# Two vector instructions of the mixing step moved behind the next remainder, in a Trainium2 transformer block

## The reference

```python
hn = rms_norm(h, norm_mlp_g[l])
u = jnp.square(jax.nn.relu(hn @ w_mlp_in[l]))   # 2048 -> 8192
h = h + u @ w_mlp_out[l]                         # 8192 -> 2048
```

## Time and profile before

| | us |
|---|---|
| median of three runs | 2722.47 |
| lowest, highest | 2721.12, 2723.18 |
| the profiled execution | 2723.25 |
| its span in the trace | 2721.5 |
| PE busy | 2560.5 (94%) |
| DVE busy | 1713.7 (63%) |
| POOL busy | 1023.0 (38%) |
| ACT busy | 976.9 (36%) |

### The profile page before, as it was taken

The page is one execution under the profiler, slowest core; times in us unless marked ns, Lnnn a source line. Parts: engine busy times, 40 slices in busy tenths (PEclk is TensorE's granted clock), DMA queues, the critical chain, the costliest instruction groups (busy, mean ns, idle before and its releaser), DMA issues.

```text
span 2721.5 us, 34691 instructions
## 1 busy us (share of the span) xinstructions
PE 2560.5 (94%) x14354; PEld 2219.9 (82%) x14354; DVE 1713.7 (63%) x1894; ACT 976.9 (36%) x1246; POOL 1023.0 (38%) x560
## 2 busy tenths in 40 slices
PE   9999999999999999997999999999789888989886
PEld 8898888888888888887999999999777666767665
DVE  5565555455333334345666665666798999899888
ACT  4445443344222223123433333333343334333434
POOL 0000000000000000017777777777756577565743
PEclk9999999999999999998999999999899999999988
DMA  7222222222323334222443334333523332322221
GB/s 246 84 88 80 92 80 88 89 82 85 101 92 100 92 100 155 94 84 70 127 129 124 125 120 137 119 124 123 224 78 140 117 131 78 139 93 113 104 85 70
DMA packets 158064, 299.49 MB, mean 110 GB/s; under 512 B 8512, under 2 KB 113104, under 8 KB 149088
## 3 DMA queue, kind: packets, MB, share of 16 engines
q1 hardware_dynamic: 157776, 297.44, 32.5%
q10 hardware_dynamic: 144, 0.02, 0.0%
HBM read 276.41 MB, written 21.01 MB: 109 GB/s over the span
## 4 chain that ended last, share of the span: by engine, by line
PE 60%; DVE 22%; issue 7%; POOL 5%; ACT 3%; DMA 1%; SPq 0%; DVEq 0%; ACTq 0%; POOLq 0%
PE bank L1473 20%; PE bank L1475 19%; PE bank L1474 19%; DVE ring L1282 8%; DVE up_lo L1214 4%; POOL down_raw L1376 4%; DVE stream L1307 2%; ACT up_hi L782 2%; DVE down_forms L1273 2%; DVE hidden_out L1237 1%; PE bank L1579 1%; ACT ring L834 1%; PE bank L1562 1%; POOL up_raw L1376 1%; DMA up_raw<-in_up_units 1%
## 5 line engine op out<-in xcount | busy, mean ns | idle before, releaser
L1376 POOL TENSOR_TENSOR up_raw<-up_raw 128x256 f32<-128x256 f32 (+1 forms) x384 | 515.1, 1345 | 194.6 <-DMA up_raw<-in_up_units 173.9
L901 DVE TENSOR_TENSOR w_lo<-landing,w_hi 128x1024 fp32r<-128x1024 f32 x200 | 248.8, 1244 | 467.4 <-ACT w_hi L593 467.2
L1376 POOL TENSOR_TENSOR down_raw<-down_raw 128x1024 f32<-128x1024 f32 x128 | 385.7, 3031 | 265.6 <-DVE ring L1282 265.6
L1282 DVE TENSOR_TENSOR ring<-down_raw,ring 128x1024 fp32r<-128x1024 f32 x224 | 439.0, 1974 | 67.3 <-ACT ring L834 66.1
L1214 DVE TENSOR_TENSOR up_lo<-up_raw,up_hi 128x1792 fp32r<-128x1792 f32 x128 | 301.3, 2354 | 244.2 <-ACT up_hi L782 244.2
L1379 POOL TENSOR_TENSOR form_raw_a<-form_raw_a 128x1024 f32<-128x1024 f32 x3 | 8.1, 2730 | 1184.9 <-DVE form_raw_a L1185 1184.9
L593 ACT ACTIVATE w_hi<-landing 128x1024 fp32r<-128x1024 f32 x200 | 212.0, 1060 | 667.5 <-PE bank L1475 663.5
L834 ACT ACTIVATE ring<-down_raw 128x1024 fp32r<-128x1024 f32 x224 | 234.0, 1058 | 464.6 <-PE bank L1475 247.6
L782 ACT ACTIVATE up_hi<-up_raw 128x1792 fp32r<-128x1792 f32 x128 | 218.0, 1703 | 437.9 <-PE bank L1475 401.7
L1473 PE MATMUL bank<-xn_hi,w_hi 128*128 128x512 f32 x928 | 367.1, 396 | 2.8 <-DVE w_lo L901 2.2
L1475 PE MATMUL bank<-xn_hi,w_lo 128*128 128x512 f32 x928 | 361.8, 390 | 0.0
(11 more groups left out here) (167 smaller groups left out, 5257.9 us busy)
## 6 DMA issues: line engine op xcount, KB each, us to landing
up_raw<-in_up_units SPq DMA_DIRECT2D x128, 512.0 KB, 3.6
down_raw<-in_down_blocks SPq DMA_DIRECT2D x64, 1024.0 KB, 6.8
landing<-in_w_in SPq DMA_DIRECT2D x72, 512.0 KB, 3.6
landing<-in_w_gate SPq DMA_DIRECT2D x64, 512.0 KB, 3.7
landing<-in_w_out SPq DMA_DIRECT2D x32, 512.0 KB, 3.6
hidden_rows<-hidden_out SPq DMA_DIRECT2D x32, 512.0 KB, 5.3
raw_forms<-hidden_rows SPq DMA_DIRECT2D x17, 512.0 KB, 10.2
landing<-in_w_branch_a SPq DMA_DIRECT2D x16, 512.0 KB, 3.4
```

The source lines that it names most:

```text
L901: nc.vector.tensor_tensor(w_lo[:, s, :], landing[:, u % LAND, :], w_hi[:, s, :].bitcast(F32), ALU.subtract).then_inc(unit_lo, 1)
L1282: nc.vector.tensor_tensor(part[:, 1, :], raw, part[:, 0, :].bitcast(F32), ALU.subtract)\
L1376: return nc.gpsimd.tensor_tensor(out, a, b, ALU.add)
```

## The change

The mixing is cut in two. `mixed_products` holds its waits and the first four instructions. `hidden` keeps the last two: the fifth subtraction (L1233 before) and the squared ReLU (L1237 before). `mixed_products` stays where the whole was, behind the remainder of unit u+2. `hidden` is issued one step of the loop later, behind the remainder of unit u+3. For the last group, in the down stage, both stand together as before. No instruction is added or taken away.

```diff
-            def hidden(s):
+            def mixed_products(s):
                 done = 5 * s
                 dve.wait_ge(up_used, up_place(s, 3) + 1)
...
                 dve.wait_ge(mixed, done + 3)
                 nc.vector.tensor_tensor(mix[:, 1:3, :], up_products(s, 2, 7, 4), mix[:, 5:7, :], ALU.add)\
                     .then_inc(mixed, 1)
-                nc.vector.tensor_tensor(mix[:, 3:4, :], fifth, mix[:, 6:7, :], ALU.subtract).then_inc(mixed, 1)
-                dve.wait_ge(mixed, done + 5)
+
+            def hidden(s):
+
+                nc.vector.tensor_tensor(mix[:, 3:4, :], up_products(s, 3, 4), mix[:, 6:7, :], ALU.subtract)\
+                    .then_inc(mixed, 1)
+                dve.wait_ge(mixed, 5 * s + 5)
                 if s:
                     dve.wait_ge(hidden_stored, 16 * s)
                 nc.vector.scalar_tensor_tensor(out=hidden_out[:], in0=mix[:, 0:4, :], scalar=0.0, in1=mix[:, 0:4, :],
...
                 if UP_ORDER[n - 2][1] == 3:
-                    hidden(UP_ORDER[n - 2][0])
+                    mixed_products(UP_ORDER[n - 2][0])
+                if n > 2 and UP_ORDER[n - 3][1] == 3:
+                    hidden(UP_ORDER[n - 3][0])
...
                     if p == 2:
+                        mixed_products(SUBS - 1)
                         hidden(SUBS - 1)
```

## The result

| | before | after |
|---|---|---|
| median of three runs, us | 2722.47 | 2698.19 |
| lowest, highest | 2721.12, 2723.18 | 2696.33, 2700.52 |
| span of the profiled execution | 2721.5 | 2698.7 |

The ratio is 0.9912, with a 95% interval of 0.989 to 0.9935: 24.3 us less.

The account below looks back on a forecast made before the run. PE was taken to bound the up stage, stalling on late DVE remainders: 18.4 us of waits, 24.9 with added cost, less 1.5, plus 1.0, gave 24.4 us off 2723.25, 2698.9 profiled; 2698 us on the median's scale, range 2694 to 2702.

Parts of the forecast that it names:

- The remainder of u+3 starts on ACT's high parts, 0.86 us earlier: Up stage, DVE: with two instructions gone ahead of it, this remainder waits for ACT, starting at 1605.93 instead of 1606.79.
- It takes 2.02 us, since POOL's sum now comes second: Remainder of u+3 starts before POOL's sum of u+5, ends at 1607.95; PE wants it at 1608.97, so the stall goes.
- Rival 1: POOL's sum of u+5 still starts first, remainder takes 3.1 us: 5 us back, 2703 us; chance 0.12.
- The moved instructions are covered: DVE behind the remainder of u+3: 0.41 + 1.40 us fit before u+4's remainder can start at 1610.95; cost 0.
- POOL's sums of u+5 end near 1603.9: POOL's three sums, each held by a DVE instruction, end near 1613.7 in the prediction's frame; ACT wants them at 1614.26.
- SP's store is the same: SP's queue: the store starts when the ReLU ends, 1609.8 to 1610.5, against 1610.22 before; its longer wait holds nobody.
- The sum, 24.4 us: Up stage total: 18.4 us of PE waits plus 25 x 0.26, less 1.5, plus 1.0 from the stretch before.
- POOL's late sums: PE's longest wait, 1.2 us, was put down to these and expected to stay: 1.2 + 0.26 us off the gain.
- a ceiling: Whole excess of both up-stage stretches, 27.0 us, which no version of this change can pass in this stage.
- the slower rival: POOL's queue past its margin in every group: 47 us lost against 24 won, 2745 us; chance 0.03.
- the priced row: ACT's wait for a late set of POOL sums, 5.01 us instead of 3.33: 1.68 us as the price of one.
- the 0.5 us of one set of sums: Margin left for POOL's sums of u+5 before ACT wants them; it was 4 us with the stall.

Follow-up runs that it names:

- run 5: Kernel before, mixing where it was, with POOL's sums of u+5 made to wait until the remainder of u+3 is done: 2700.89 us (0.9914).
- run 8: Changed kernel with POOL's first sum of u+5 made three times, 2 x 1.3 us more of POOL per group: 2751.82 us (1.0098).
- run 6: Changed kernel, POOL's first sum of u+4 made twice: 2708.72 us; second kernel also leaves out one block's sum in three units per group: 2698.84 us.

## Why the prediction was right

It forecast 2698 us, and the changed kernel came to 2698.19 and, a second time, 2697.49. Step by step:

- *The remainder of u+3 starts on ACT's high parts, 0.86 us earlier:* right, with 0.90 us of idle DVE ahead of it. The run with the ReLU alone moved shows that this is all the change needs.
- *It takes 2.02 us, since POOL's sum now comes second:* right, and decisive. The old order with POOL held gives nearly the whole gain; the old amount of mixing in one place, one unit later, gives nothing. The stall of 1.01 us was 0.86 us late plus 1.09 held, less the 1.02 in hand, and 0.1 us between the first two matmuls behind it. Taking either away ends it: the hold in run 5, the lateness in run 8, where a remainder on time was held for 1.05 us and cost 0.13. That is why 0.86 us of earlier start is worth a whole stall. (By the starts in the earlier trace rows the remainder was 0.78 us late and POOL's sum 0.21 us ahead of it; the prediction's 0.86 and 0.29 count from the end of the squared ReLU, 0.08 us later. Nothing hangs on it.)
- *Rival 1* (the remainder of u+3 still held) did not come about: it took 2.02 or 2.03 us in all 28 groups of the first profile.
- *The moved instructions are covered:* right. They ended at 1600.37, where I had 1600.7 in this frame. The margin was thin: one more squared ReLU there cost 15.2 us in the stretch.
- *POOL's sums of u+5 end near 1603.9* (in this frame): too late by 2.1 us, they ended at 1601.79. The third sum came ahead of the remainder of u+4, and not behind it. The mistake was harmless: the remainder paid 0.5 us of its margin.
- *SP's store is the same:* right for its issue. Its landing I left out: the median went from 5.3 to 2.9 us, and the load of u+6 is now issued some 2 us ahead of it and not right beside it. The other runs fit that: 5.3 us with POOL held, where load and store are issued together, 2.9 with all six moved, where they aren't.
- *The sum, 24.4 us:* its size was off. The stage gave 27.0 us in the first pair and 27.2 in the second. The term is "25 waits with 0.26 us each, less one of POOL's". It left out what the list of waits doesn't hold of the stretch's excess: PE was late at u+3 in 27 of the 28 groups, where the list has 25 waits in all. And it kept 1.5 us for POOL's late sums that were not POOL's. The longest wait, 1.2 us, is that of unit 118, whose remainder begins at 1881.55, is held to 3.11 us and is a u+3 like the others; the unit behind POOL's late sums cost only 0.4 us. All of it went. The excess of 27.0 us, which I had taken for a ceiling, was the value. The first pair's medians show 24.3 us; the second time, against the kernel before as timed beside it, they show 26.6.
- That 24.3 us was measured where 24.4 had been worked out was therefore partly luck: the sum was 2.6 us short of what the stage gives. In the first pair of profiles 4.2 us of the stage's 27.0 don't reach the span, 2.9 of them at the start of the up stage, at a granted clock of 0.82 instead of 0.87. The forecast lies between the first pair's 22.8 us of span and the second's 27.5.

Of the slower rival, the priced row (1.68 us for a late set of sums) was of the right order: two extra sums cost 1.88 us per group and lose to the kernel before. But its margin was measured by the wrong thing. From the 0.5 us of one set of sums that I worked out, or the 2.7 us that the first profile shows (they end at 1601.79, and ACT takes them at 1604.46), one can't tell where losses begin; the runs put that at about 0.9 us of added POOL work per group, and the point where the whole gain is lost between 1.3 and 2.6 us.

## What to carry to other kernels

When a stall is the sum of two delays less a margin, taking out either delay is worth the whole stall, as long as the other is not much longer than the margin (1.05 us held against 1.0 in hand cost 0.13). So work out the margin first, and put the work that can wait (here a squared ReLU, wanted only by a store) behind the instruction that PE wants next, but no more of it in one place than the gap there holds. Here the excess of a stretch over its back-to-back time was a better forecast (27.0 us, measured 27.0 and 27.2) than the sum of the waits in the list (24.4).

## What the runs showed of the hardware

- An engine's waits are not its room. POOL waited 2.8 us per group for its loads, and 1.3 us more work already made it the bound, with waits down to 0.2 us in the whole stretch. A POOL sum that comes second to a DVE instruction with both inputs in SBUF is stretched (2.44 us beside the remainder, 1.29 alone): POOL's busy time went from 467.5 to 555.6 us for 28 sums that take 1.3 us alone, 36 us.
- In the rows of this case, the instruction that starts first runs on, and the other takes nearly as much longer as the first still needs. For the remainder of 2.02 us, the time still needed and the time added were 1.23 and 1.09 us in the kernel before, 0.63 and 0.49 in the changed kernel, 0.34 and 0.20 in the second kernel of run 6. The squared ReLU, 1.3 to 1.4 us without such a start, took 1.86 with 0.78 us still to go. The rule cited in the prediction (the Trainium skill, "SBUF — State Buffer", section "SBUF: two separate sides") agrees. The five mixing instructions, which read one input from PSUM, took the same 0.41 to 0.69 us with a POOL sum beside them and without.
- Who comes first at the port is decided within a tenth of a us: a sum begun 0.11 us ahead of the remainder of u+4 held it for 0.5 us, in all 28 groups of the first profile and 27 of the second.
